# Moving two context blocks, the row order and one weight load in a 512-row gather kernel

## The chip, the cores and the metric

One core of one Trainium2 chip. The metric is the device time of one execution in microseconds (us). TensorE is called PE, VectorE DVE, ScalarE ACT, GpSimd POOL and SyncE SP, as in the profile.

## The reference, cut to what matters

Two model blocks run one after the other on 256 tokens of width 1024. The first ends with a PEER layer: each token and head picks 16 experts, and for each of them a row of `u_tab` and a row of `v_tab` are fetched. The second block has two streams, the latent `x` and a context `ctx`, and a gated feed-forward layer (`_conv_ffn`) whose weights both streams share.

```python
def _peer(h, w_q, sub_keys, u_tab, v_tab):
    ...
    def block_fn(args):
        tb, ib, gb = args
        u = u_tab[ib]
        act = jax.nn.gelu(jnp.einsum("td,thkd->thk", tb, u).astype(jnp.float32), approximate=False)
        vv = v_tab[ib]
        return jnp.einsum("thk,thkd->td", (gb * act).astype(vv.dtype), vv)

def _conv_ffn(h, w_up, conv_w, conv_b, w_down):
    u = h @ w_up
    up = jnp.pad(u, ((0, 0), (1, 1), (0, 0)))
    u = up[:, :-2] * conv_w[0] + up[:, 1:-1] * conv_w[1] + up[:, 2:] * conv_w[2] + conv_b
    a, v = jnp.split(u, 2, axis=-1)
    return (jax.nn.silu(a) * v) @ w_down
```

## The kernel before

**The gathers.** The PEER layer is 512 indirect DMAs issued by POOL (line 3099). Each brings 128 table rows of 4 KB (0.524 MB) into one of `NR = 12` ring buffers; below, one such DMA is called a row. There are 256 u rows (two token tiles of 128) and 256 v rows (eight segments of 32; the first 128 belong to token tile 0). The list `ROWS` (`fetched`, line 365) sets their order. A buffer is used again when its row has been consumed: a u row by one DVE dot product (`tensor_tensor_reduce`, line 2031), v rows by PE. PE takes v rows of tile 0 two at a time and those of tile 1 four at a time (`beside_others`); here a *v group* is four v rows of tile 1, taken by eight 512-column matmuls.

**What is woven into them.** `woven` (line 461) walks through the row order on PE, DVE and ACT alike, and at places counted in rows it advances a second program, `context()`, by one step. `step_places` (line 484) is the table of these places. A row is consumed 11 rows after it is issued, and six counts come ahead of the first row, so a step at place P comes when the rows up to number P - 18 have been consumed.

**The context program.** It computes the context stream's pool mixer and feed-forward layer and, as the weights are in SBUF anyway, the first 119 tokens of x as well. A *visit* is one 128-wide block of the up-projection (two halves of 8 matmuls), its three-tap convolution (ACT line 2442 for the middle tap, then four DVE operations of `conv_up`, line 1651), a SiLU on ACT and a product on DVE. There are three kinds of visit in this stretch: `ctx` (256 context columns), `a` (120 columns of x) and `both` (377 columns, context and x at once). The `a` columns exist only when token tile 0 has finished the PEER layer: v row 128 consumed, the sum added (`v_add`), then normalised, pooled and normalised again. That part is `first_half()` below. So the first `EARLY_BLOCKS` blocks are visited twice, as `ctx` before and as `a` after it, and the other blocks once, as `both`. After the 22 blocks comes the down-projection (`cd`, 24 steps), then the context's key and value projection (weights `kvc`), and after the last v row the remaining 138 columns of x ("stage b").

In the kernel before, `ctx` visits 0 to 7 stand at places 178 to 269, `first_half()` at 292 to 316, the eight `a` visits at 318 to 334, the 14 `both` visits at 336 to 420, and `cd` at 428 to 498. `BESIDE` lists steps of `first_half()` beside which visits stand; it is empty.

**Loads.** SP issues the weight loads in program order into three slots of 2 MB and waits, before each, for the work that last used the slot. `kvc` (line 703) is behind the last down-projection load and ahead of a wait for the end of the down-projection (`p_cd`, 24).

Of the kernel before, what the change touches and what calls it, by code (L numbers as in the profile page):

```python
# [96 lines left out]
def program(nc, a, out):  # L97
# [2 lines left out]
    MUL, ADD, SUB, MAX, MIN, BYP = ALU.mult, ALU.add, ALU.subtract, ALU.max, ALU.min, ALU.bypass  # L100
    ctx = ExitStack()

    EARLY_BLOCKS, BESIDE = 8, ()

    GOES_ON = {
        "p_gp": ("p_hT", 4), "p_h2T": ("p_gp", 1), "p_xc": ("p_h2T", 4), "p_zb": ("p_xc", 4), "p_xT": ("p_zb", 1), "p_zbb": ("p_xT", 2), "p_xTb": ("p_zbb", 1), "p_cum": ("p_g", 1), "p_crow": ("p_cum", 1),
# [24 lines left out]
    def at(name, n):  # L131

        sem = S[name]
        while name in GOES_ON:
            name, before = GOES_ON[name]
            n += before
        return sem, n
# [168 lines left out]
    FIRST_B, BEFORE_A = 22 + EARLY_BLOCKS, EARLY_BLOCKS - len(BESIDE)  # L306
# [57 lines left out]
    AHEAD = 40  # L364

    def fetched():


        u = [("u", n // 128, n % 128) for n in range(256)]
        v = [("v", s, n) for s in range(8) for n in range(32)]  # L370
        first = [x for g in range(0, 128 - AHEAD, 4) for x in v[g:g + 4] + u[AHEAD + g:AHEAD + g + 4]]
        g0 = 128 - AHEAD
        first += [x for g in range(5) for x in v[g0 + 8 * g:g0 + 8 * g + 8] + u[128 + 4 * g:132 + 4 * g]]
        then = [x for g in range(20) for x in v[128 + 4 * g:132 + 4 * g] + u[176 + 4 * g:180 + 4 * g]]
        return u[0:AHEAD] + first + u[148:176] + then + v[208:]

    ROWS = fetched()
    NTH = {x: n for n, x in enumerate(ROWS)}

# [104 lines left out]
    def step_places():  # L484

        places = [5 * (k + 1) // 2 for k in range(11)] + [44 + 56 * (k - 10) // 10 for k in range(11, 34)]
        n = 178
        for f in range(BEFORE_A + 2):
            places.append(n)
            n += 13 if f < BEFORE_A else 2  # L490
        n = max(n, 292)
        for lengths in ([1.9] * 14, [2.3] * EARLY_BLOCKS, [6.4] * (22 - EARLY_BLOCKS), [1] * 2,
                        ([3.3] * 8 + [2.4] * 4) * 2, [1] * 11):
            for length in lengths:
                places.append(int(n))
                n += length
        return places
# [9 lines left out]
    def woven(peer, context):  # L507


        n, steps, half = 0, 0, None  # L510
        places = step_places()
        for what in peer:
            if what == "rest":
                n += 1
                if n == half:
                    next(context, None)
                    half = None
                elif steps < len(places) and n >= places[steps]:
                    steps += 1
                    if next(context, None) == "half":  # L520
                        half = n + 3
        for _ in context:
            pass
# [107 lines left out]
    def _(sp):  # L631
        free, count, nth = [None] * 4, [0] * 4, [0]

        def load(name, until, *parts, n=4, slot=None):

            i = nth[0] % n if slot is None else slot
            nth[0] += 1
            for signal in free[i] or ():
                sp.wait_ge(*at(*signal))
            for put, src in parts:  # L640
                sp.dma_start(put(slots[i]), src).then_inc(S[f"d_w{i}"], 16)
                count[i] += 16
            free[i] = until if isinstance(until, list) else [until]
            ready[name] = S[f"d_w{i}"], count[i], slots[i]

        def kcols(w, c0, n):
            return ((lambda ap: ap[:, 0:8 * n].rearrange("p (k c) -> p k c", k=8)),
                    w[:, c0:c0 + n].rearrange("(k p) c -> p k c", p=128))
# [8 lines left out]
        def down(l, half, f0, nf):  # L657
            w = a["ffn_w_down_2"][l]
            return ((lambda ap: ap[:, 0:512 * nf].rearrange("p (f c) -> p f c", f=nf)),
                    w[128 * f0:128 * (f0 + nf), 512 * half:512 * half + 512].rearrange("(f p) c -> p f c", p=128))  # L660
# [42 lines left out]
        for half in range(2):  # L703
            for q, (f0, nf) in enumerate(((0, 8), (8, 8), (16, 6))):
                load(("cdn", half, q), ("p_cd", 4 * (3 * half + q) + 4), down(0, half, f0, nf), n=3)
        load("kvc", ("p_ckv", 3), kcols(a["attn_w_qkv_2"][0], 1024, 512), n=3)
        sp.wait_ge(*at("p_cd", 24))
        sp.dma_start(cl[:, 0:512], a["c_late"][:, 0:512]).then_inc(S["d_l"], 16)
        sp.dma_start(hpC[:, 0:1568], a["c_bands"]).then_inc(S["d_l"], 16)
        sp.dma_start(nfb, a["normf_g"].partition_broadcast(128)).then_inc(S["d_g2"], 16)  # L710
        nth[0] = 0
        sp.wait_ge(*at("p_v", 248))
        load("pool", ("p_pl", 4), pool_w(), n=3)
# [916 lines left out]
    def _(ve):  # L1630
# [381 lines left out]
        def peer():  # L2012
            for what in turns():
# [9 lines left out]
                elif what[0] == "use" and ROWS[what[1]][0] == "u":  # L2023
                    n = what[1]
                    _, t, m = ROWS[n]
                    j, k = 8 * t + m // 16, m % 16
                    if j > 1 and k == 0:
# [1137 lines left out]
```

## Time and profile before

| | |
|---|---|
| median of 2 runs | 1694.42 us (1694.03 to 1694.82) |
| the profiled execution | 1694.82 us |
| its span | 1693.0 us, so 1.8 us lie around it |
| stretch of the gathers | first issue at 312.93 us, last at 1191.26 us |
| mean granted PE clock | 0.94 |

In the profile every f32 matmul of the program stands as two PE instructions, so one visit of 16 matmuls is x32. A timeline row merges neighbours of one form. PE times overlap a little at the seams. Times inside the program are counted from the start of the span.

### The profile page before, as it was taken

What the parts mean: (1) busy time and instruction counts of PE and PEld (TensorE: products, weight loads), DVE (VectorE), ACT (ScalarE), POOL (GpSimd) and SP (SyncE); (2) the same over time, 40 slices, a digit from 0 to 9 for tenths busy, and PEclk for the clock granted to TensorE, in tenths of its full rate; (3) what the DMA queues carried; (4) which work ended last, traced back from release to release, by engine and by line L of the source; (5) the groups of instructions that cost most, each with busy time, mean ns of one, the idle gap of its engine ahead of it and who ended that gap; (6) DMA issues with size and microseconds to landing.
All of it is one profiled execution on the core that took longest, in us unless ns stands there. A gap on an engine that the chain in (4) does not pass through costs nothing.

```text
span 1693.0 us, 22384 instructions
## 1 busy us (share of the span) xinstructions
PE 1464.2 (86%) x8446; PEld 1037.2 (61%) x8446; DVE 1041.1 (61%) x2200; ACT 530.3 (31%) x836; POOL 748.3 (44%) x676
## 2 busy tenths in 40 slices
PE   8999999827676769743999989998699999999999
PEld 7997675824121334323755545555399986699987
DVE  4865633897597866489787774401244157568864
ACT  6653331211121121132331220003233164466652
POOL 0025220477677777675566556643100013027650
PEclk9999999978778889876999999998899999999999
DMA  7447860799999999998999999986768756635451
GB/s 277 150 150 314 320 225 25 261 396 332 399 400 385 375 391 405 394 402 306 361 398 401 370 353 359 372 320 237 250 219 278 265 215 264 211 138 188 174 194 43
DMA packets 160267, 487.40 MB, mean 288 GB/s; under 512 B 10144, under 2 KB 13984, under 8 KB 156960
## 3 DMA queue, kind: packets, MB, share of 16 engines
q0 software_dynamic: 73728, 268.47, 41.4%
q1 hardware_dynamic: 86432, 217.51, 35.2%
q8 instruction: 67, 1.10, 0.3%
q14 instruction: 40, 0.33, 0.1%
HBM read 484.89 MB, written 1.05 MB: 287 GB/s over the span
## 4 chain that ended last, share of the span: by engine, by line
PE 55%; DVE 15%; DMA 9%; POOL 7%; issue 6%; ACT 2%; DVEq 0%; ACTq 0%; POOLq 0%
PE ps L764 54%; POOL arena L3099 6%; DMA arena<-in_peer_v,cl 5%; DVE arena L2031 4%; DMA arena<-in_peer_u,arena 3%; DVE arena L1645 2%; PE ps L768 2%; DVE wring L2031 1%; DVE arena L1651 1%; POOL wring L3099 1%; DVE cbase L1651 1%; ACT arena L2442 1%; DVE arena L1648 1%; DMA wring<-in_peer_u,arena 1%; DMA wring<-in_attn_w_qkv 0%
## 5 line engine op out<-in xcount | busy, mean ns | idle before, releaser
L764 PE MATMUL ps<-arena,wring 128*32 128x512 f32 (+6 forms) x3016 | 697.9, 467 | 111.0 <-DMA arena<-in_peer_v,cl 77.8
L764 PEld LDWEIGHTS ps<-arena,wring 128*128 128x128 f32 (+1 forms) x3016 | 395.5, 171 | 396.4 <-DMA arena<-in_peer_v,cl 138.6
L3099 POOL DMA_INDIRECT arena<-in_peer_u,arena x206 | 236.2, 1147 | 218.4 <-DVE arena L1988 77.4
L2031 DVE CUSTOM_DVE_ANT_0 arena<-arena 128x1024 f32<-128x1024 f32 x206 | 246.7, 1225 | 122.8 <-DMA arena<-in_peer_u,arena 119.7
L3099 POOL DMA_INDIRECT arena<-in_peer_v,cl x222 | 240.1, 1081 | 132.7 <-issue 59.4
L2442 ACT ACT_TABLE_LOAD x71 | 91.1, 1283 | 355.6 <-DVE arena L2031 178.2
L1651 DVE SCALAR_TENSOR_TENSOR cvs<-ps,vec,cvs 128x255 f32<-128x255 f32 (+3 forms) x236 | 104.5, 443 | 55.2 <-ACT cvs L2442 47.9
L764 PE MATMUL ps<-hhl,wh 128*128 128x256 f32 (+1 forms) x528 | 126.2, 322 | 0.6 <-POOL hhl L3109 0.4
L764 PEld LDWEIGHTS ps<-arena 128*128 128x128 f32 (+1 forms) x708 | 87.6, 196 | 45.9 <-issue 27.5
L1645 DVE TENSOR_TENSOR wl<-wring,wh 128x2048 fp32r<-128x2048 f32 (+1 forms) x42 | 92.5, 2202 | 37.0 <-ACT wh L2445 36.1
L764 PE MATMUL ps<-arena 128*128 128x128 f32 (+4 forms) x708 | 99.1, 293 | 18.3 <-DVE arena L1648 6.4
L3053 POOL TENSOR_TENSOR arena<-arena,cl 128x256 f32<-128x256 f32 x56 | 43.8, 782 | 158.0 <-PE ps L764 154.7
L2445 ACT ACTIVATE wh<-wring 128x2048 fp32r<-128x2048 f32 (+1 forms) x44 | 82.6, 1878 | 70.7 <-PE ps L764 36.7
L764 PE MATMUL ps<-ahl,wh 128*128 128x512 f32 (+1 forms) x320 | 103.0, 347 | 0.1
L2445 ACT ACTIVATE arena<-ps 128x512 f32<-128x512 f32 (+1 forms) x97 | 56.0, 578 | 145.1 <-PE ps L764 105.1
L764 PE MATMUL ps<-hhl,wl 128*128 128x256 f32 x352 | 99.2, 282 | 0.0
L764 PEld LDWEIGHTS ps<-hhl,wh 128*128 128x128 f32 x528 | 87.8, 190 | 9.8 <-POOL hhl L3109 1.3
L2442 ACT ACTIVATE arena<-arena 128x16 f32<-128x16 f32 (+3 forms) x60 | 35.4, 591 | 182.3 <-DVE arena L2031 57.2
L764 PE MATMUL ps<-sqb,wring 128*128 128x138 f32 (+1 forms) x736 | 89.5, 285 | 2.1 <-ACT xT L2442 2.1
L764 PEld LDWEIGHTS ps<-sqb,wring 128*128 128x128 f32 x736 | 88.5, 193 | 3.0 <-issue 2.3
L2442 ACT ACTIVATE cvs<-ps,vec 128x256 f32<-128x256 f32 (+3 forms) x118 | 62.9, 533 | 80.4 <-PE ps L764 65.5
L3125 POOL TENSOR_TENSOR wl<-wring,wh 128x2048 fp32r<-128x2048 f32 x3 | 13.7, 4574 | 160.9 <-ACT wh L2445 160.7
(279 smaller groups left out, 2208.9 us busy)
## 6 DMA issues: line engine op xcount, KB each, us to landing
wring<-in_ups SPq DMA_DIRECT2D x37, 2048.0 KB, 9.7
wring<-in_ada SPq DMA_DIRECT2D x24, 2048.0 KB, 10.1
wring<-in_ffn_w_down SPq DMA_DIRECT2D x12, 2048.0 KB, 7.8
wring<-in_w_in SPq DMA_DIRECT2D x8, 2048.0 KB, 8.3
wring<-in_ffn_w_down SPq DMA_DIRECT2D x6, 1536.0 KB, 6.8
wring<-in_peer_wq SPq DMA_DIRECT2D x4, 2048.0 KB, 15.8
wring<-in_attn_w_qkv SPq DMA_DIRECT2D x4, 2048.0 KB, 8.5
wring<-in_w_out SPq DMA_DIRECT2D x2, 2048.0 KB, 9.3
```

Of the source, the lines that this page charges most:

```text
L764: return pe.matmul(o, l, r, start=start, stop=stop)
L768: return pe.transpose(o, i, ident[0:n, 0:n])
L1645: return ve.tensor_tensor(o, x, y, op)
L1648: return ve.tensor_scalar(o, x, s1, s2, op0, op1)
L1651: return ve.scalar_tensor_tensor(o, x, s, y, op0, op1)
L2031: ve.tensor_tensor_reduce(out=o, in0=o, in1=h2[:, t, :], scale=1.0, scalar=0.0, op0=MUL, op1=ADD, accum_out=dots[j % 2][:, k:k + 1]).then_ ...
L2442: return ac.activation(o, x, f, bias=bias, scale=scale, accum_out=accum)
L2445: return ac.activation(o, x, ACT.Copy)
L3053: k = po.tensor_tensor(OTs[l % 2][:, m:m + 2, :], AM[:, m:m + 2, :], bc(cl[:, o:o + 128], 2, 1), MUL)
L3099: po.indirect_dma_start(out=ring[n % NR], out_offset=None, in_=table, in_offset=bass.IndirectOffsetOnAxis(ap=which, axis=0)).then_inc(S[f" ...
L3125: told(po.tensor_tensor(lo.bitcast(FR), src, hi, SUB), *split_done(n))
```

## The change

It does four things. (1) The row order is regular: after the first 40 u rows it alternates 4 v rows and 4 u rows until the u rows end, and 40 v rows are left. Before, there was a piece with 8 v rows to 4 u rows and then 28 u rows alone, and 48 v rows were left. (2) Two more blocks are early ones: 10 `ctx` and 10 `a` visits, 12 `both` visits. (3) Four of the `ctx` visits (6 to 9) stand beside steps 0, 1, 8 and 9 of `first_half()`; the table of places is changed for that: `ctx` 0 to 5 at places 178 to 278, `first_half()` at 311 to 326, `a` at 327 to 348, `both` at 350 to 421, `cd` at 430 to 498. (4) The load `kvc` is issued after the wait for the end of the down-projection and three small loads.

```diff
-    EARLY_BLOCKS, BESIDE = 8, ()
+    EARLY_BLOCKS, BESIDE = 10, (0, 1, 8, 9)
...
-        first = [x for g in range(0, 128 - AHEAD, 4) for x in v[g:g + 4] + u[AHEAD + g:AHEAD + g + 4]]
-        g0 = 128 - AHEAD
-        first += [x for g in range(5) for x in v[g0 + 8 * g:g0 + 8 * g + 8] + u[128 + 4 * g:132 + 4 * g]]
-        then = [x for g in range(20) for x in v[128 + 4 * g:132 + 4 * g] + u[176 + 4 * g:180 + 4 * g]]
-        return u[0:AHEAD] + first + u[148:176] + then + v[208:]
+        both = [x for g in range(0, 256 - AHEAD, 4) for x in v[g:g + 4] + u[AHEAD + g:AHEAD + g + 4]]
+        return u[0:AHEAD] + both + v[256 - AHEAD:]
...
-            n += 13 if f < BEFORE_A else 2
-        n = max(n, 292)
+            n += 20 if f < BEFORE_A else 2
+        n = max(n, 311)
...
-        load("kvc", ("p_ckv", 3), kcols(a["attn_w_qkv_2"][0], 1024, 512), n=3)
         sp.wait_ge(*at("p_cd", 24))
         sp.dma_start(cl[:, 0:512], a["c_late"][:, 0:512]).then_inc(S["d_l"], 16)
         sp.dma_start(hpC[:, 0:1568], a["c_bands"]).then_inc(S["d_l"], 16)
         sp.dma_start(nfb, a["normf_g"].partition_broadcast(128)).then_inc(S["d_g2"], 16)
+        load("kvc", ("p_ckv", 3), kcols(a["attn_w_qkv_2"][0], 1024, 512), n=3)
```

PE's order around `first_half()` before. 32x512 is a matmul on a v row, 128x256 (x16) a `ctx` visit, the 128x120 rows on `cbase` and `wring` x16 belong to `first_half()`, and 128x120 x16 per visit after them are the `a` visits:

```order
L764 MATMUL ps<-arena,wring 32x512 x28
L764 MATMUL ps<-arena,cbase 128x120 x4
L768 MATMUL ps<-cbase,arena 128x128 x8
L764 MATMUL ps<-arena 128x136 x8
L764 MATMUL ps<-arena,wring 128x120 x16
L768 MATMUL ps<-cbase,gt 128x128
L764 MATMUL ps<-arena,cbase 128x120 x8
L768 MATMUL ps<-cbase,wt 128x128
L764 MATMUL ps<-arena,wring 128x120 x48
L764 MATMUL ps<-arena,wring 32x512 x8
```

The same piece of PE's order in the changed kernel:

```order
L761 MATMUL ps<-arena,cbase 128x120 x4
L761 MATMUL ps<-arena,wring 128x256 x32
L765 MATMUL ps<-cbase,arena 128x128 x8
L761 MATMUL ps<-arena 128x136 x8
...
L761 MATMUL ps<-arena,wring 128x120 x8
L761 MATMUL ps<-arena,wring 128x256 x16
L761 MATMUL ps<-arena,cbase 128x120 x8
L761 MATMUL ps<-arena,wring 128x256 x16
L761 MATMUL ps<-arena,wring 32x512 x8
L761 MATMUL ps<-arena,wring 128x120 x48
```

Two whole `ctx` visits now stand between the first piece of `first_half()` and its transposes, and one on either side of its last sum; a v group stands behind them.

SP's order at the end of the down-projection, before:

```order
L641 DMA wring<-in_ffn_w_down 128x6x512
L641 DMA wring<-in_attn_w_qkv 128x8x512
L708 DMA cl<-in_c_late 128x512
L709 DMA arena<-in_c_bands 128x1568
L710 DMA arena<-in_normf_g 128x1024
```

and in the changed kernel:

```order
L638 DMA wring<-in_ffn_w_down 128x6x512
L704 DMA cl<-in_c_late 128x512
L705 DMA arena<-in_c_bands 128x1568
L706 DMA arena<-in_normf_g 128x1024
L638 DMA wring<-in_attn_w_qkv 128x8x512
```

The 2 MB of `in_attn_w_qkv` (`kvc`) have moved behind the wait that stands at `in_c_late` and behind that load and the next two.

## Rows read from the trace of the kernel before

**Rows 1.** The page: engine totals, and clock and DMA share in 40 slices.

```profile
PE 1464.2 (86%) x8446; PEld 1037.2 (61%) x8446; DVE 1041.1 (61%) x2200; ACT 530.3 (31%) x836; POOL 748.3 (44%) x676
...
PEclk9999999978778889876999999998899999999999
DMA  7447860799999999998999999986768756635451
```

**Rows 2.** Windows: busy time of each engine in seven stretches.

```profile
core 0: us, PE busy (x) PEld busy (x) DVE busy (x) ACT busy (x) POOL busy (x), PEclk, DMA share, GB/s
590.70:731.00 140.30, 104.02 (x426) 51.63 (x424) 86.30 (x210) 22.72 (x35) 99.90 (x94) 0.91 1.02 395
731.00:743.00 12.00, 11.19 (x31) 2.09 (x30) 9.14 (x26) 4.48 (x8) 8.95 (x11) 0.82 1.03 406
743.00:799.40 56.40, 17.06 (x83) 15.24 (x82) 54.25 (x133) 17.67 (x39) 36.53 (x29) 0.64 0.92 339
799.40:835.00 35.60, 34.92 (x288) 31.63 (x288) 27.53 (x78) 11.47 (x21) 16.50 (x15) 0.94 0.95 343
835.00:1000.00 165.00, 163.34 (x616) 87.02 (x617) 128.36 (x292) 44.44 (x69) 101.06 (x90) 1.00 1.01 388
1000.00:1144.10 144.10, 139.75 (x547) 73.32 (x549) 52.18 (x105) 4.38 (x8) 81.80 (x80) 0.99 0.94 347
1144.10:1202.00 57.90, 42.53 (x218) 23.08 (x222) 7.41 (x15) 14.32 (x26) 19.71 (x21) 0.91 0.74 269
```

**Rows 3.** The chain that ended last, inside first_half: start us, us, what.

```profile
784.19 3.52 DVE arena L2031 x7
...
788.53 2.38 DVE arena L2031 x4
```

**Rows 4.** Timeline of PE: one ctx visit, then the matmuls of first_half.

```profile
669.58 7.08 PE L764 MATMUL ps<-arena,wring 128*128 128x256 f32 x32
...
743.07 1.15 PE L764 MATMUL ps<-arena,cbase 128*128 128x120 f32 x8
756.99 1.97 PE L768 MATMUL ps<-cbase,arena 128*128 128x128 f32 x8 [12.77 <-DVE arena L1648]
...
784.04 3.74 PE L764 MATMUL ps<-arena,cbase 128*128 128x120 f32 x16 [2.23 <-ACT arena L2442]
```

**Rows 5.** DVE in 743 to 799.4 us, by line: busy, mean ns.

```profile
L2031 DVE CUSTOM_DVE_ANT_0 arena<-arena 128x1024 f32<-128x1024 f32 x22 | 26.1, 1223 | 0.4
L2031 DVE CUSTOM_DVE_ANT_0 wring<-wring,arena 128x1024 f32<-128x1024 f32 x4 | 4.8, 1226 | 0.1
```

**Rows 6.** Timeline of DVE: product and taps of ctx visits.

```profile
732.36 0.43 DVE L1645 TENSOR_TENSOR arena<-cvs 128x256 f32<-128x256 f32 x1 [1.69 <-ACT cvs L2442]
733.56 2.04 DVE L1651 SCALAR_TENSOR_TENSOR cbase<-ps,vec,cbase 128x255 f32<-128x255 f32 x4 [0.77 <-ACT cbase L2442]
```

**Rows 7.** PE by form, 799.4 to 835 us (a visits), then 835 to 1000 us.

```profile
L764 PE MATMUL ps<-arena,wring 128*128 128x120 f32 x256 | 31.4, 287 | 7.6 <-ACT arena L2442 7.6
...
L764 PE MATMUL ps<-arena,wring 128*128 128x377 f32 x438 | 142.3, 482 | 0.7 <-DMA wring<-in_ups 0.7
```

**Rows 8.** The page's DMA issues: the up-projection weights, KB each, us to landing.

```profile
wring<-in_ups SPq DMA_DIRECT2D x37, 2048.0 KB, 9.7
```

**Rows 9.** Timeline of PE behind the down-projection: a v group, the first key projection.

```profile
1150.81 1.92 PE L764 MATMUL ps<-arena,wring 128*32 128x512 f32 x16
1159.61 10.02 PE L764 MATMUL ps<-arena,wring 128*128 128x256 f32 x32 [6.87 <-issue]
```

**Rows 10.** Timeline of SP's queue: the kvc load and the last load behind the wait.

```profile
1098.33 0.37 SPq L641 DMA_DIRECT2D wring<-in_attn_w_qkv  x1
...
1144.97 0.65 SPq L710 DMA_DIRECT2D arena<-in_normf_g  x1
```

**Rows 11.** DMA view, 1144.1 to 1202 us: share in 40 slices, one issue and its us to landing.

```profile
DMA  9999999999999300000000389986899899999999
...
arena<-in_normf_g SPq DMA_DIRECT2D x1, 512.0 KB, 11.2
```

More of the change, by code:

```diff
@@ L489, in step_places @@
             places.append(n)
-            n += 13 if f < BEFORE_A else 2
-        n = max(n, 292)
-        for lengths in ([1.9] * 14, [2.3] * EARLY_BLOCKS, [6.4] * (22 - EARLY_BLOCKS), [1] * 2,
-                        ([3.3] * 8 + [2.4] * 4) * 2, [1] * 11):
+            n += 20 if f < BEFORE_A else 2
+        n = max(n, 311)
+        for lengths in ([1.2] * 14, [2.3] * EARLY_BLOCKS, [6.4] * (22 - EARLY_BLOCKS), [1.5] * 2,
+                        ([3.2] * 8 + [2.4] * 4) * 2, [1] * 11):
             for length in lengths:
```

## The prediction

> **What bounds the kernel now.** I read the page's totals and slices first. PE is busy 86% of the span, and where its clock falls, around 340 to 480 us and again near 760 to 800 us, the DMA share is high: the gathers, not PE, set the pace there [rows 1]. Then the windows, cut at the borders of the steps [rows 2]. They show four regimes. Up to 743 us the DMA engines are full (share 1.02 and 1.03, 395 to 406 GB/s), and PE has slack: 104 of 140 us. From 743 to 799.4 us, the steps of first_half, PE works 17.06 of 56.4 us at a clock of 0.64, the DMA share falls to 0.92 with 339 GB/s, and DVE is busy 54.25 us: DVE is the bound. From 799.4 to 1144.1 us (a visits, both visits, down-projection) PE is busy 338.0 of 344.7 us: PE is the bound, and what counts there is the amount of matmul work. In the last stretch, up to the last v row at about 1202 us, PE and DMA alternate.
>
> The chain of waits agrees for the second regime: it runs through u row products on DVE, one behind the other [rows 3]. There are 26 of them in that stretch, 30.9 us of DVE's 54.25 [rows 5], since 28 u rows stand alone there. PE meanwhile has four waits between short pieces, the longest 12.77 us for DVE's scaled rows [rows 4].
>
> **Part 1, where first_half starts: +21 us.** It needs the last v row of tile 0 and place 292 or 311. Counted in ROWS, that v row is number 271 before and number 291 after, 20 rows later. Up to it DMA is the bound in both kernels: the windows show 395 GB/s, so a row of 0.524 MB costs 1.33 us, and 20 rows 26.5 us. Against that, SP has fewer loads to make before that point. Before, the slots allow one load of the last two early weight pairs, the pool weights and two pairs for both visits; after, both remaining early pairs and the pool weights, but no pair for later, as these slots are freed only by ctx visits 6 to 9. That is one load of 2.1 MB less, 5.3 us. Net 26.5 - 5.3 = +21.2, and first_half starts at 743 + 21 = 764 us. Bounds: 0 (if the two ctx visits taken away from here had held it back; PE's slack speaks against it) and 30 (20 rows at the 1.5 us a row of the windows' 94 issues in 140.3 us). The two ctx visits that leave this stretch save nothing: PE has 36 us of slack in it.
>
> **Part 2, the length of first_half: -3 us.** PE's own 17.06 us remain. The four ctx visits at 7.08 us each [rows 4] add 28.3 us. Placed end to end that is 45.4 us, the lower bound; if nothing overlapped, 56.4 + 28.3 = 84.7 us, the upper. On DVE the 26 u products shrink to about 9, as only 16 places pass and half the rows are v rows: -17 x 1.19 = -20 us. Taps and product of a ctx visit add 2.04 + 0.43 us [rows 6], four times 9.9 us. So DVE falls to about 44 us and is no longer alone the bound. Step by step: PE does its first 1.15 us, then visits 6 and 7, 15 us, which covers the 12.77 us wait almost exactly. Transposes, windows and pool matmuls follow, waiting for DVE and ACT by turns, to about 26 us; visit 8, sum, visit 9 bring PE to about 42 us. Behind visit 9 stand ACT's middle tap, DVE's 2.04 us of taps, then the reciprocal and eight scalings and ACT's eight shifts before the first a visit may start, since DVE takes the taps of visit 9 ahead of the scalings: about 11 us of PE waiting are left. I take 53 us against 56.4, nearest to the lower bound because the two long waits are covered: -3.4 us. The a visits start at 764 + 53 = 817 us instead of 799.4.
>
> **Part 3, the PE-bound stretch: -17 us.** Two more a visits: 31.4 us for eight is 3.92 us each [rows 7], +7.8 us. Two both visits fewer: 142.3 us for 438 instructions is 0.325 us, times 32 is 10.4 us a visit [rows 7], -20.8 us. v groups consumed between the first a visit and the end of the down-projection: 24 before (rows 307 to 479), 22 after (315 to 479, without 471), as two of them fall into first_half, where PE waits anyway. At 1.92 us [rows 9] that is -3.8 us. The down-projection itself does not change. Sum -16.8 us. Bounds: -22 (ten a visits in 34 us, since some of the eight ran while the clock was still at its lower level; it averages 0.94 there [rows 2]) and 0 (the loads below come late). DMA has room over the whole stretch: about 170 rows and 28 MB of weights, 117 MB, need 296 us at 395 GB/s, and PE needs 327.
>
> The weights of the a visits are the cover that gets thin. The pair for a visits 2 and 3 and that for 4 and 5 are issued only when visit 9 has left PE, about 11 us before the first a visit; the first of them is wanted 8 us after that, the second after another 10 us. The median load of this kind lands in 9.7 us [rows 8], about half of these gaps, so I cost it at nothing, and at up to 10 us if gathers fill the DMA engines at that time.
>
> **Part 4, the kvc load: +6 us.** Before, it is issued at 1098.33 us, long before its first use at 1159.61 us [rows 9, 10]. After, it stands behind p_cd 24 and three loads, so behind 1144.97 us [rows 10]; in front of it the 512 KB gain takes 11.2 us to land, at 1156.2 us [rows 11]. The DMA engines are full until about slice 13 of that window, 1163 us, and then stand idle for 12 us [rows 11]. With 2.1 MB more, 5.2 us at 405 GB/s, they empty at about 1168.5 us, and the load is in by then: PE waits 0 to 9 us beyond 1159.6. I take 6. PE is in order: behind this wait stand the v groups whose buffers the last 12 gathers need, so all of the wait goes to the end. The wait also keeps nothing back on SP: the pool weights behind it are gated by p_v 248 later on.
>
> The Trainium skill says in "DMA: Bandwidth & Descriptors", section "Queues, rings and completion order", that each DMA engine alternates between the queues that have work. By that rule kvc would have half of the 405 GB/s from 1156.2 us on, an estimate of 10.4 us, landing at 1166.6 us, a wait of 7 us; the full drain gives 9, and an undisturbed load none. The trace shows only the totals here.
>
> **The sum.** +21.2 - 3.4 - 16.8 + 6 = +7.0 us. On the profiled execution, 1694.8 us (span 1693.0 and 1.8 around it), that is 1701.8; that execution lies 0.4 us above the median, so 1701.
>
> **The rivals.**
>
> Filled better (faster). first_half shrinks to about 45.4 us (every wait covered), kvc lands in time, and the a visits run at full clock. Then the terms are +21.2 - 11 - 19 + 0 = -9: 1686 us. For it: PE's waits are in fact the 39 us that four visits of 7.08 us fit into. Against: taps of visit 9 stand ahead of the scalings on DVE, and the load has only 15 us between issue and use.
>
> Low clock in first_half (slower than before). In the stretch 743 to 799.4 us the granted clock is 0.64, so most of it at the lower level, 1.2 GHz [rows 2]. If the ctx visits placed there run at that level too, they take 14 us each instead of 7: +28 us, of which the 11 us wait behind visit 9 absorbs some. first_half is then about 70 us, and the result 1701 + 17 = 1718 us. It decides from the point where PE's waits between the pieces stay long enough for the clock to stay down. For it: even in the 12 us ahead of first_half the clock averages only 0.82. Against: two visits stand back to back for 14 us, and from 799.4 us on, with PE busy throughout, the clock averages 0.94, then 1.00 [rows 2].
>
> The Trainium skill's page "TensorE: Matmul & The Clock Gate", section "HAM oscillation — how this bites in real kernels", holds that waits between short bursts of matmuls put the next burst back to half rate. By that rule first_half of the kernel before is such a case, which its 0.64 bears out, and the new order stands between the two cases: this rival's 1718 us, or the forecast.
>
> Weights late in the a visits (slower). Five pairs, 10.5 MB, and the rows from about 320 to 350 and those refilling the ring, 28 rows or 14.7 MB, fall between visit 9 and the first both visit. At 395 GB/s that is 64 us, where PE needs 11 + 39 + 6 = 56 us. Then 8 to 10 us more: 1710 us. Against: DMA had a share of only 0.95 in the same stretch before.
>
> Nothing moved: the start of first_half shifts less than 21 us because the 8 to 4 piece was itself held up by DVE; worth at most 10 us, in the forecast's range.
>
> **How the numbers follow.** The forecast (net of a later start, a filled gap and a late load) has 0.5, its own range 1694 to 1707 us. Filled better has 0.25, 1680 to 1693. Weights late 0.12, low clock 0.13. 1684 to 1718 leaves out about 0.1 on either side. A measurement of this kernel can tell about 2% (34 us) from no change. Faster by more than that, under 1660.5 us, would need all of first_half's idle and the late start gone at once: 0.04. Slower, over 1728.3 us, needs low clock and late weights together: 0.04. Within 2%: 0.92.
>
> **What would show it.** In the profile of the changed kernel: the first 128x120 matmul on cbase near 764 us, not 743; 128x256 visits in the gap behind it at about 7 us each (14 would be the low clock); the first a visit near 817 us; waits for `wring<-in_ups` inside the a visits under 3 us in total; the first both visit near 865 us, the end of the down-projection near 1145 us; and a wait for `wring<-in_attn_w_qkv` of about 6 us ahead of the key projection. If first_half starts before 755 us or lasts under 48 us, parts 1 or 2 are wrong and the time falls below 1694.

## The result, and the profile after

The changed kernel takes 1717.45 us (median of 2 runs, 1716.17 to 1718.74) where the kernel before takes 1694.42. The ratio is 1.0146, 95% interval [1.0115, 1.0177]: 23 us slower, inside the 2% that counts as no change, but three times the 7 us of the forecast and almost at the end of its range. The profiled execution took 1717.8 us, with a span of 1715.9.

Totals, clock and DMA share on the page of the kernel after, to be held against [rows 1]. The totals say nothing: PE has 2.7 us more, in 23 us more of span. The 7 and the 6 that the clock had in the eighteenth and nineteenth slice are now 8 and 9: first_half is filled.

```profile
PE 1466.9 (85%) x8510; PEld 1041.6 (61%) x8510; DVE 1043.7 (61%) x2210; ACT 533.2 (31%) x843; POOL 742.4 (43%) x676
...
PEclk9999999968798888989899999998999999999999
DMA  7438851799999999997999997975758757545551
```

Windows of the kernel after, cut at the same steps as [rows 2]: up to first_half; first_half; the a visits; both visits and down-projection; up to the key projection; from there to shortly before the last v rows.

```profile
core 0: us, PE busy (x) PEld busy (x) DVE busy (x) ACT busy (x) POOL busy (x), PEclk, DMA share, GB/s
590.70:766.60 175.90, 115.38 (x405) 47.64 (x406) 126.46 (x307) 25.99 (x40) 130.58 (x124) 0.84 1.03 402
766.60:820.70 54.10, 41.62 (x242) 33.97 (x241) 38.30 (x100) 23.22 (x48) 20.19 (x19) 0.93 0.82 293
820.70:873.60 52.90, 46.62 (x369) 41.71 (x369) 40.09 (x101) 17.78 (x37) 26.33 (x23) 0.91 1.01 375
873.60:1158.50 284.90, 277.94 (x1049) 148.36 (x1053) 157.51 (x348) 41.19 (x60) 160.37 (x150) 0.98 0.93 350
1158.50:1184.70 26.20, 7.39 (x49) 3.71 (x46) 7.11 (x14) 7.73 (x11) 8.40 (x9) 0.74 0.95 360
```

Ahead of first_half the DMA engines are still full (1.03) and PE still has slack, 60 us of it. In first_half PE now works 41.6 of 54.1 us at a clock of 0.93, where it was 17.06 of 56.4 at 0.64; DMA falls to 0.82. The a visits take 52.9 us with the DMA engines full again.

The timeline of PE in the kernel after, first_half to the first both visit. The two ctx visits at the start of first_half run end to end, 14.0 us, and cover the old wait of 12.77 us; behind the last of them PE waits 10.34 us for ACT. Two waits for up-projection weights follow, one inside the a visits and one ahead of the first both visit.

```profile
766.57 1.06 PE L761 MATMUL ps<-arena,cbase 128*128 128x120 f32 x8
767.46 13.99 PE L761 MATMUL ps<-arena,wring 128*128 128x256 f32 x64
...
799.64 1.94 PE L761 MATMUL ps<-arena,cbase 128*128 128x120 f32 x16
801.41 8.94 PE L761 MATMUL ps<-arena,wring 128*128 128x256 f32 x48
820.70 27.08 PE L761 MATMUL ps<-arena,wring 128*128 128x120 f32 x210 [10.34 <-ACT arena L2439]
...
859.22 10.89 PE L761 MATMUL ps<-arena,wring 128*128 128x120 f32 x80 [2.80 <-DMA wring<-in_ups]
873.58 2.16 PE L761 MATMUL ps<-arena,wring 128*128 128x377 f32 x4 [3.48 <-DMA wring<-in_ups]
```

Further on, still PE of the kernel after: the first key projection and the stage that follows the last v row.

```profile
1165.19 1.92 PE L761 MATMUL ps<-arena,wring 128*32 128x512 f32 x16
1184.66 9.00 PE L761 MATMUL ps<-arena,wring 128*128 128x256 f32 x32 [17.55 <-DMA wring<-in_attn_w_qkv]
...
1233.68 3.97 PE L761 MATMUL ps<-arena 128*128 128x136 f32 x16 [6.29 <-DVE arena L1645]
```

In the kernel before that last stage starts at 1209.42 us and the key projection at 1159.61 [rows 9]. Six marks hold the whole story (start times on PE, us; the down-projection by its end):

| | first_half | a visits | first both visit | down-projection ends | key projection | stage after the last v row |
|---|---|---|---|---|---|---|
| before | 743.1 | 799.4 | 835.0 | 1144.1 | 1159.6 | 1209.4 |
| after | 766.6 | 820.7 | 873.6 | 1158.5 | 1184.7 | 1233.7 |
| stage, after less before | +23.5 | -2.3 | +17.3 | -24.2 | +10.7 | -0.8 |

The last line is the change of the stretch that ends at each mark (the first one: of all that lies ahead of first_half). It adds up to 24.2 us; the spans differ by 22.9.

### The profile page after: what moved, and what is told of

Same layout as the page of the kernel before. It is cut to its first block, busy times and chain, and to the rows that moved or that the text cites. A ratio compares the mean times of both kernels' runs of the same rounds, so it can differ in the third digit from the quotient of the medians.

```text
span 1715.9 us, 22539 instructions
## 1 busy us (share of the span) xinstructions
PE 1466.9 (85%) x8510; PEld 1041.6 (61%) x8510; DVE 1043.7 (61%) x2210; ACT 533.2 (31%) x843; POOL 742.4 (43%) x676
## 4 chain that ended last, share of the span: by engine, by line
PE 57%; DMA 11%; POOL 10%; DVE 9%; issue 5%; ACT 2%; SPq 0%; DVEq 0%; ACTq 0%; POOLq 0%
PE ps L761 56%; POOL arena L3096 8%; DMA arena<-in_peer_v,cl 3%; DMA wring<-in_peer_v,cl 2%; POOL wring L3096 2%; DMA arena<-in_peer_u,arena 2%; DVE arena L2028 2%; DMA wring<-in_ups 2%; PE ps L765 1%; DMA wring<-in_attn_w_qkv 1%; DVE arena L1642 1%; DVE arena L1648 1%; ACT arena L2439 1%; DMA wring<-in_peer_u,arena 1%; DVE cbase L1648 0%
## 5 line engine op out<-in xcount | busy, mean ns | idle before, releaser
L761 PEld LDWEIGHTS ps<-arena,wring 128*128 128x128 f32 (+1 forms) x3048 | 404.6, 173 | 422.9 <-DMA arena<-in_peer_v,cl 169.2
L3096 POOL DMA_INDIRECT arena<-in_peer_u,arena x214 | 243.7, 1139 | 256.8 <-PE ps L761 117.0
L2028 DVE CUSTOM_DVE_ANT_0 arena<-arena 128x1024 f32<-128x1024 f32 x214 | 256.9, 1224 | 123.3 <-DMA arena<-in_peer_u,arena 120.0
L3096 POOL DMA_INDIRECT arena<-in_peer_v,cl x214 | 231.6, 1082 | 131.4 <-issue 59.2
```

The lines of the kernel that those rows point to most:

```text
L761: return pe.matmul(o, l, r, start=start, stop=stop)
L2028: ve.tensor_tensor_reduce(out=o, in0=o, in1=h2[:, t, :], scale=1.0, scalar=0.0, op0=MUL, op1=ADD, accum_out=dots[j % 2][:, k:k + 1]).then_ ...
L3096: po.indirect_dma_start(out=ring[n % NR], out_offset=None, in_=table, in_offset=bass.IndirectOffsetOnAxis(ap=which, axis=0)).then_inc(S[f" ...
```

## The experiments

Sixteen runs of fifteen kernels (one kernel ran twice) stand in four sets; each set shares its runs of the kernel before, whose medians were 1704.9, 1697.0, 1694.8 and 1696.9 us. Absolute times are compared inside a set only, ratios across them. Two words for what follows: "kvc early" means the load in its place of before, and a "place" is a number in the step table, by which steps are spread over the list of rows.

**First set: the parts of the change by themselves.** Theory A came from the marks: the late kvc load and the later start of first_half make the loss, while the ten early blocks give something back. Its rival C was that the visits inside first_half lose.

The kernel before with the kvc load moved behind the wait, and nothing else:

```diff
-        load("kvc", ("p_ckv", 3), kcols(a["attn_w_qkv_2"][0], 1024, 512), n=3)
         sp.wait_ge(*at("p_cd", 24))
...
         sp.dma_start(nfb, a["normf_g"].partition_broadcast(128)).then_inc(S["d_g2"], 16)
+        load("kvc", ("p_ckv", 3), kcols(a["attn_w_qkv_2"][0], 1024, 512), n=3)
```

> The kernel before with part 4 alone: kvc issued behind the wait for the end of the down-projection and the three small loads. Theory A (the load's lateness is on the path, since PE's wait for it holds back the v groups and with them the last gathers): PE waits 15 to 18 us ahead of the key projection instead of 6.9, and the time is 9 to 12 us longer, 1704 to 1707. Rival B (the end is set by gathers and the wait is hidden): within 2 us of before, 1693 to 1697.

Ratio 1.006 [1.0037, 1.0084], 10 us. The wait ahead of the key projection, in the timeline of PE of this kernel:

```profile
1173.65 6.72 PE L764 MATMUL ps<-arena,wring 128*128 128x256 f32 x21 [18.59 <-DMA wring<-in_attn_w_qkv]
```

18.59 us instead of 6.87, and the 11.7 us more go to the end almost whole.

The kernel after with that one line back in its old place:

> The changed kernel with part 4 undone: kvc issued ahead of the wait, as before. Theory A: 1717.5 minus 9 to 12, 1705 to 1709, of which the rest over before comes from the later start. Rival B: 1716 to 1719.

Ratio 1.0084 [1.0052, 1.0117], 0.6% under the 1.0146 of the kernel after. The same price from the other side. The wait at the key projection is back to what it was:

```profile
1189.07 3.33 PE L761 MATMUL ps<-arena,wring 128*128 128x256 f32 x7 [6.88 <-issue]
```

The kernel before with the regular row order and the places that go with it, but 8 early blocks, none in first_half, kvc early:

```diff
-        first = [x for g in range(0, 128 - AHEAD, 4) for x in v[g:g + 4] + u[AHEAD + g:AHEAD + g + 4]]
...
-        return u[0:AHEAD] + first + u[148:176] + then + v[208:]
+        both = [x for g in range(0, 256 - AHEAD, 4) for x in v[g:g + 4] + u[AHEAD + g:AHEAD + g + 4]]
+        return u[0:AHEAD] + both + v[256 - AHEAD:]
...
-        n = max(n, 292)
+        n = max(n, 311)
-        for lengths in ([1.9] * 14, [2.3] * EARLY_BLOCKS, [6.4] * (22 - EARLY_BLOCKS), [1] * 2,
-                        ([3.3] * 8 + [2.4] * 4) * 2, [1] * 11):
+        for lengths in ([1.2] * 14, [2.3] * EARLY_BLOCKS, [6.4] * (22 - EARLY_BLOCKS), [1.5] * 2,
+                        ([3.2] * 8 + [2.4] * 4) * 2, [1] * 11):
```

> The kernel before with the regular row order and the table of places that it needs (first_half at 311, its steps 1.2 apart, down-projection as in the changed kernel), still 8 early blocks, all ctx visits ahead of first_half, kvc early. Theory A (first_half waits for the last v row of tile 0, 20 rows later, and what is lost there is only partly won back by fewer u products inside it): first_half starts near 766 us, lasts 38 to 42 us, so the a visits start near 806 us instead of 799, and the time is 1696 to 1702. Rival C (the visits placed in first_half and their late weights cause the loss, the order does not): 1690 to 1695.

Ratio 0.9949 [0.993, 0.9968]: faster than before, and than either theory had it, though first_half starts 20 places later. Theory A's account of the late start fell here. first_half took 36 us (before: 56.4), and, what nobody had counted on, the stretch from the key projection to the stage after the last v row took 31.8 us where the kernel before takes 49.8.

The kernel before with the other half of the change, `EARLY_BLOCKS, BESIDE = 10, (0, 1, 8, 9)`, and the old row order:

> The kernel before with part 2 and 3 of the change alone: 10 early blocks, ctx visits 6 to 9 beside steps 0, 1, 8 and 9 of first_half, everything else (row order, table's numbers, kvc) as before. Theory A: first_half starts at 743 us as before, takes about 64 us as DVE is its bound and gets 10 us more, and the PE-bound stretch is 13 us shorter: 1684 to 1692. Rival C (visits in first_half cost more than they cover, by late weights): 1698 to 1710.

Ratio 1.01 [1.0065, 1.0135], slower, as rival C had it. first_half took 83 us. It still held the 28 u rows that stand alone in the old order, and the four visits came on top, with waits of 8.59, 6.79, 5.11 and 8.02 us between the pieces. The new order does not rescue the four visits either: 1.0084 with both against 0.9949 with the order alone.

**Second set: the number of early blocks or their place?**

The kernel after, kvc early, `EARLY_BLOCKS, BESIDE = 8, (0, 1, 8, 9)`:

> The kernel after with the kvc load early and with 8 early blocks instead of 10, all four visits still placed inside first_half (BESIDE stays). Theory P (the place is what costs: visits inside first_half lengthen DVE's and ACT's line there and free the weight slots late, so that the a visits start late and run slowly): the ratio to before stays at 1.005 to 1.015, first_half lasts 50 us or more. Theory N (the number is what costs: two more early blocks need more visits ahead of first_half and two more a visits): the ratio falls to that of the kernel with the order alone, 0.995, within 0.003.

Ratio 0.9984 [0.9968, 1.0001]. The same, `10, ()` and 12 places between the visits:

> The kernel after with the kvc load early, 10 early blocks, and BESIDE empty: all ten ctx visits stand ahead of first_half, 12 places apart. Theory P (place): PE has slack there and two both visits (20.8 us) become two a visits (7.8 us), so it is faster than the order alone: ratio 0.985 to 0.993. Theory N (number): the ten visits hold the stretch ahead of first_half up, ratio 1.003 or more.

Ratio 0.9993 [0.998, 1.0006]. The kernel before with ten blocks ahead of first_half, 11 places apart:

> The kernel before with 10 early blocks, 11 places apart instead of 13, all ahead of first_half, first_half still at place 292, the old row order. Theory P: 8 to 13 us faster than before, ratio 0.992 to 0.996. Theory N: no faster, ratio 0.999 or more.

Ratio 0.9984 [0.9967, 1.0001]. And the kernel after (kvc late) with `8, ()` and 13 places:

> The kernel after (kvc late) with 8 early blocks ahead of first_half and BESIDE empty, so that the row order, its places and the late kvc load are what is left of the change. If the parts add, it has the order's 0.995 and kvc's 0.006: 1.001, between 0.998 and 1.004. If the late kvc load costs more with the new order, because the last v groups come later there, 1.005 or more.

Ratio 0.9996 [0.9981, 1.0011]; less the load's 0.006 that is 0.994, near the 0.9949 of the order alone, so these two parts add. Neither theory P nor theory N held. The place costs 0.35% (0.9984 against 0.9949), the number 0.45% (0.9993), and both together 1.35% (1.0084), more than their sum; the last of these ratios comes from the first set, the other two from the second.

Why the number costs anything was the riddle: by the marks of the kernel with ten blocks ahead of first_half, the down-projection ends at 1148.2 us, 6.8 us ahead of the one with eight (1155.0), and yet its last stage comes no earlier (1213.4 and 1212.9 us), although its kvc load is early and the other's late. The kernel before with ten blocks shows it best, in its windows: first_half, the a visits, both visits and down-projection, the rest up to the stage after the last v row.

```profile
749.00:808.70 59.70, 17.68 (x84) 16.03 (x83) 57.37 (x138) 18.07 (x40) 36.10 (x29) 0.58 0.92 342
808.70:859.80 51.10, 46.11 (x369) 41.21 (x369) 42.04 (x115) 16.28 (x33) 25.43 (x24) 0.92 0.98 361
859.80:1134.80 275.00, 273.30 (x1048) 145.98 (x1048) 163.37 (x360) 41.41 (x63) 162.78 (x151) 1.00 0.99 376
1134.80:1207.80 73.00, 52.21 (x257) 24.59 (x257) 11.43 (x24) 17.30 (x32) 27.46 (x30) 0.94 0.82 302
```

The down-projection ends at 1134.8 instead of 1144.1 us, 9.3 us earlier, and the last window grows from 65.3 to 73.0, in which PE works only 52. The gain is given back to waits for rows.

**Third set: what the tail waits for.** The timeline of POOL of the kernel before, which issues the gathers, holds the cause. The first row of a run of four gathers names what it waited for:

```profile
1152.99 0.94 POOL L3099 DMA_INDIRECT arena<-in_peer_v,cl  x1 [2.14 <-PE ps L764]
...
1156.74 0.94 POOL L3099 DMA_INDIRECT arena<-in_peer_v,cl  x1 [0.30 <-issue]
1175.19 0.94 POOL L3099 DMA_INDIRECT arena<-in_peer_v,cl  x1 [17.50 <-PE ps L764]
...
1182.55 0.94 POOL L3099 DMA_INDIRECT arena<-in_peer_v,cl  x1 [2.69 <-PE ps L764]
...
1191.26 0.94 POOL L3099 DMA_INDIRECT arena<-in_peer_v,cl  x1 [0.31 <-issue]
```

Behind 1156.74 us no buffer is free until PE, in its order, is through the key projection and the v group behind it: 17.5 us without an issue. Twelve gathers are still to come after that, and PE ends up waiting for them. Its waits between the key projection and the last stage, in the kernel before:

```profile
PE ps L764 <- DMA arena<-in_peer_v,cl: 6.5, 7, 1.6
PE ps L764 <- DMA wring<-in_peer_v,cl: 0.7, 1, 0.7
```

That is 7.2 us in eight waits. How many are left is set by the place at which the down-projection ends, and that is a sum of the table. The order alone ends it at place 509 (311 + 14 x 1.2 + 8 x 2.3 + 14 x 6.4 + 2 x 1.5 + 70.4), the kernel after at 501, since two both visits of 6.4 fewer and two a visits of 2.3 more are 8 places. The kernel before ends it at 501 too, by its own table (292 + 14 x 1.9 + 8 x 2.3 + 14 x 6.4 + 2 x 1 + 72). Theory G: this, not the matmul work, decides.

The kernel before with one number changed:

```diff
-        for lengths in ([1.9] * 14, [2.3] * EARLY_BLOCKS, [6.4] * (22 - EARLY_BLOCKS), [1] * 2,
+        for lengths in ([1.9] * 14, [2.3] * EARLY_BLOCKS, [7.0] * (22 - EARLY_BLOCKS), [1] * 2,
```

> The kernel before with the both visits 7.0 places apart instead of 6.4: the down-projection ends at place 508 instead of 500, and nothing else changes. Theory G (the gathers set the end of this stretch; PE finishes the down-projection early and then waits while the last v rows come): with 8 rows fewer left behind the key projection, the stretch from the key projection to the stage after the last v row falls from 49.8 to 30 to 40 us, while the end of the down-projection moves by at most 8 us; ratio 0.993 to 0.998. Theory M (PE's matmul work from 799 to 1144 us sets the end, as in the prediction): v groups only change their place, ratio 0.999 to 1.003.

Ratio 0.9949 [0.9932, 0.9966]. The whole gain of the new order, from one number. PE of this kernel, key projection and last stage, then the first and the last of POOL's last four gathers:

```profile
1167.87 9.48 PE L764 MATMUL ps<-arena,wring 128*128 128x256 f32 x32 [6.88 <-issue]
...
1189.83 4.21 PE L764 MATMUL ps<-arena,wring 128*32 128x512 f32 x32
1199.98 2.38 PE L764 MATMUL ps<-arena 128*128 128x136 f32 x9 [5.94 <-DVE arena L1648]
```

```profile
1182.91 0.94 POOL L3099 DMA_INDIRECT arena<-in_peer_v,cl  x1 [16.98 <-PE ps L764]
...
1186.63 0.93 POOL L3099 DMA_INDIRECT arena<-in_peer_v,cl  x1 [0.31 <-issue]
```

The key projection comes 8.3 us later (8 more rows are used ahead of it), four gathers are left instead of twelve, and from there to the last stage it is 32.1 us instead of 49.8. The gap on POOL is as long as it was, but little is left behind it. PE has no wait for rows in this stretch any more, and its busy time there falls by 10.5 us (36.64 to 26.16), of which two v groups less are 3.8; the rest is not accounted for.

The kernel after, with 7.1 in the place of 6.4:

> The kernel after with the both visits 7.1 places apart instead of 6.4, so that the down-projection ends at place 509 instead of 501; the rest of the change stays, the late kvc load too. Theory G: the two both visits taken away brought the down-projection's end 8 places forward, and the rows left over come behind it; given back, the ratio falls from 1.0146 to about 1.010. Theory M: the same ratio as after, within 0.002.

Ratio 1.0072 [1.0052, 1.0091]: half of the change's loss was this, and more than theory G had forecast (1.010). The down-projection ends 4.2 us later (1162.7), the last stage comes 13.4 us earlier (1220.3).

New order, kvc early, ten blocks all ahead of first_half, 7.1:

> The kernel with the new row order, kvc early, ten ctx visits ahead of first_half (ratio 0.9993 with 6.4) and the both visits 7.1 places apart. Theory G: 4 to 8 us less, ratio 0.994 to 0.997. Theory M: 0.998 to 1.001.

Ratio 0.9927 [0.9908, 0.9946], 1682.05 us against 1694.79, faster than both kernels of this case and the fastest that ran. From 0.9993 that is 0.66%, some 11 us where theory G had 4 to 8: its direction holds, its size was again too small. And the order alone once more, to see whether its gain hung on the chip:

> The same kernel as the one with the regular row order and its places alone (8 early blocks, BESIDE empty, kvc early), on another chip. If its 0.9949 was no accident of that chip: 0.992 to 0.997. An accident: 0.999 or more.

0.9945 [0.9928, 0.9962]; it did not.

Theory G in all eighteen traces (the stretch is from the key projection to the last stage; "gathers left" are those that POOL issues after the key projection has begun; some of these kernels come in the fourth set):

| kernel | down-projection ends at place | gathers left | stretch, us |
|---|---|---|---|
| before with ten blocks ahead of first_half | 492 | 20 | 57.4 |
| before with ten blocks, four inside first_half | 492 | 20 | 55.2 |
| before; the same with kvc late | 501 | 12 | 49.8; 48.7 |
| after; the same with kvc early | 501 | 12 | 49.0; 49.4 |
| new order, ten blocks ahead of first_half | 501 | 12 | 49.7 |
| before with 7.0 | 509 | 4 | 32.1 |
| after with 7.1 | 509 | 4 | 32.0 |
| new order, eight blocks (two runs; with kvc late) | 509 | 4 | 31.8 and 31.7; 31.3 |
| new order, eight blocks, four inside first_half | 509 | 4 | 31.7 |
| new order, ten blocks, 7.1 (none, two, two or four inside first_half) | 509 | 4 | 32.0, 31.7, 32.0, 32.0 |
| new order, ten blocks, 7.8 | 518 | 0 | 30.2 |

The stretch follows the gathers left and hardly anything else that was varied, neither the row order nor the number of blocks, the place of the visits or the kvc load. It does not follow them in proportion: from 4 to 12 it grows by 17 to 18 us, from 12 to 20 by only 6 to 8.

**Fourth set: which visits inside first_half cost.** All with the new order, kvc early, ten blocks and 7.1. All four inside:

> The kernel after with the kvc load early and the both visits 7.1 places apart: of the change, the row order, ten early blocks and the four visits inside first_half are left. If the parts add (1.0072 for the wide one, less 0.006 for the load): ratio 0.999 to 1.003. What remains above the 0.9927 of the same kernel with all ten visits ahead of first_half is the price of the place of the visits.

Ratio 1.0004 [0.999, 1.0018], so the place of four visits is worth 0.77% here. Only the two at the start of first_half (`(0, 1)`, 15 places between the others):

> As the one with kvc early and 7.1, but only visits 8 and 9 inside first_half, at its first two steps, and eight ahead of it, 15 places apart. Theory W (a visit inside first_half costs where nothing waits: these two fall into the wait of 10 us for DVE's scaled rows, which they cover): first_half lasts 36 to 44 us, ratio 0.992 to 0.996. Theory S (each visit inside first_half costs about the same, for PE has slack ahead of it and none in it): half of the price, ratio 0.995 to 0.999.

Ratio 0.9938 [0.9922, 0.9955]. Only the two at its end (`(8, 9)`):

> As the one before, but visits 8 and 9 at first_half's last steps, beside and behind the sum. Theory W: here is the price: the wait for ACT ahead of the first a visit stays at 10.3 us, the one for DVE's scaled rows comes back, first_half lasts 45 to 52 us, ratio 0.998 to 1.002. Theory S: half of the price, 0.995 to 0.999.

Ratio 0.9961 [0.9949, 0.9973]. The first two are nearly free (0.11% above 0.9927, within the intervals), the last two cost 0.34%. Theory W had length and ratio of the first kernel and the waits and the length of the second, but not its ratio (0.998 to 1.002); that one lies in the range of theory S. So W holds in its direction, and not in its size. PE's timeline of the kernel with `(8, 9)` has both waits, the one that is not covered any more and the one that these visits make.

```profile
780.71 1.97 PE L765 MATMUL ps<-cbase,arena 128*128 128x128 f32 x8 [9.69 <-DVE arena L1645]
...
819.47 2.91 PE L761 MATMUL ps<-arena,wring 128*128 128x120 f32 x12 [10.34 <-ACT arena L2439]
```

With `(0, 1)` the first is almost gone, and the second is only 6.45 us:

```profile
786.34 1.09 PE L765 MATMUL ps<-cbase,arena 128*128 128x128 f32 x8 [0.58 <-DVE arena L1645]
...
811.10 1.21 PE L761 MATMUL ps<-arena,wring 128*128 128x120 f32 x4 [6.45 <-ACT arena L2439]
```

first_half lasts 33.3 us with no visit in it, 40.2 with the first two, 49.5 with the last two, 54.2 with four, and it starts only 1.6, 2.5 and 3.6 us earlier for them. Together they cost more (0.77%) than one by one (0.11 and 0.34%); by the traces the surplus does not arise in first_half (20.9 us longer for 6.9 and 16.2) but behind it: from the first a visit to the end of the down-projection it is 342.4 us with four visits inside, 340.6 with none, and 339.6 and 337.8 with two. Why is open. The windows of the four-visit kernel show the DMA engines at 0.80 and 284 GB/s over the longer first_half, so that more loads and rows are left for the stretch behind; that this is the reason is not shown:

```profile
768.90:823.10 54.20, 41.70 (x242) 34.05 (x241) 38.40 (x100) 23.22 (x48) 20.19 (x19) 0.95 0.80 284
```

Last, the fastest version with 7.8 instead of 7.1, so that the down-projection ends near place 518:

> The version that is fastest so far (new row order, kvc early, ten visits ahead of first_half, both visits 7.1 apart: 0.9927) with 7.8 instead, so that the down-projection ends at place 517 and all rows are gathered by then. Theory G (the gathers set the end): the tail behind the key projection loses nothing more, since its 32 us are PE's own work by then; ratio 0.991 to 0.995. If there were still rows to gain: under 0.990. If PE now waits for rows inside the down-projection: 0.996 or more.

Ratio 0.9936 [0.9916, 0.9956], no different from 0.9927. The last gather is issued at 1161.32 us, ahead of the key projection at 1171.04. Once four gathers or fewer are left, PE's own 30 to 32 us are the tail.

## Why the prediction was wrong, by its own steps

**Part 1, the start of first_half: right.** Forecast +21.2, measured +23.5 (766.6 for 764). What it was added up from stood too: 301 gathers were issued from 312 us to first_half instead of 281, and five loads of up-projection weights instead of six.

**Part 2, its length: right as a number.** 54.1 us for 53; -2.3 for -3.4. The steps stood too: visits at 7.0 us and full clock, the 12.77 us wait covered, "about 11 us of PE waiting" behind the last visit, 10.34 measured. DVE had 9 u products in it, as forecast. The low-clock rival is out: the stretch has 0.93, and 1.00 over the first two visits (767.4 to 781.5 us). That its 1718 us is the measured time is an accident. But the comparison misled. That first_half did not grow against 56.4 looked like four visits for nothing. The new order without them has a first_half of 33 to 36 us; the change won some 20 us there and spent them again on visits that PE's slack ahead of first_half had carried for next to nothing. The fourth set prices that at 0.77%.

**Part 3, the PE-bound stretch: this step failed first.** Forecast -16.8, measured -6.9 (17.3 - 24.2). Its terms give the a visits 35.6 + 7.8 = 43.4 us and what follows -20.8 - 3.8 = -24.6. The mark of 865 us for the first both visit was reckoned wrong, for 817 + 43.4 is 860.4. Measured are 52.9 us and -24.2: of the 9.9 us that are missing, 9.5 lie in the a visits, and the saving behind them nearly came. PE in the a visits of the kernel after, by form:

```profile
L761 PE MATMUL ps<-arena,wring 128*128 128x120 f32 x320 | 41.2, 296 | 13.1 <-ACT arena L2439 10.3 <-DMA wring<-in_ups 2.8
...
L761 PE MATMUL ps<-arena,wring 128*128 128x377 f32 x1 | 0.6, 584 | 3.5 <-DMA wring<-in_ups 3.5
```

The waits for weights are 2.80 + 3.48 = 6.3 us where the kernel before has 0.7, so 5.6 of the 9.5 us. Another 2.0 are the ten visits' own time, 41.2 for 39.2: behind its wait of 10.34 us PE runs the first 9.3 us of them at a granted clock of 0.68, where the kernel before has 0.80 over the first 10.6 us, behind a wait of 7.59. The last 1.9 are a third v group in this stretch where there were two (48 instructions of 128x512 for 32); counted where it stands, it leaves the stretch behind 2.3 us short of its saving.

The term that failed is "I cost it at nothing" for the weight loads. It rested on a median landing time of 9.7 us over the whole program [rows 8]. In the very stretch of interest the DMA view of the kernel after says:

```profile
wring<-in_ups SPq DMA_DIRECT2D x5, 2048.0 KB, 26.3
```

and that of the kernel before, from 799.4 to 835 us, had said already:

```profile
wring<-in_ups SPq DMA_DIRECT2D x4, 2048.0 KB, 20.2
```

Two and three times the median of the page, and the waits came to 6.3 us, not "under 3". They are not those that the prediction looked at. The two pairs that wait for visit 9 were issued from 808.53 us on, landed after 11.4 and 21.5 us, and came in time. Late are two that were issued inside the a visits, at 840.11 and 847.26 us: they landed after 19.1 and 26.3 us, at 859.2 and 873.6, where PE's two waits end. Nor do they hang on the visits inside first_half: with the new order and ten visits ahead of it the same waits come to 8.5 and 8.7 us (6.4 and 7.1 places), with the kernel before and ten blocks to 5.0. The rival of late weights had the right account: 64 us from the end of visit 9 to the first both visit, for 56 in the forecast. It was 63.2 us (810.4 to 873.6), at a DMA share of 1.01, and the rival's chance of 0.12 was too small.

**Part 4, the kvc load: right mechanism, size too small.** Forecast +6, measured +10.7 in the trace (17.55 us of waiting for 6.87), and 0.6% in two experiments from both sides (0.5% and 0.7% between two more pairs of kernels that differ in it alone). Full drain had been put at 9 us and was the right case, but 6 was taken: the DMA engines stayed full until about 1183 us, and the load was in at 1184.6. From the DMA view of the kernel after:

```profile
wring<-in_attn_w_qkv SPq DMA_DIRECT2D x1, 2048.0 KB, 24.7
```

The load was issued at 1159.88 us, behind three others on its own queue, of which the last landed at 1170.4 us; eight more gathers were issued meanwhile, from 1160.56 to 1171.12 us. The Trainium skill's rule that a DMA engine alternates between its queues packet by packet ("DMA: Bandwidth & Descriptors", "Queues, rings and completion order") stands behind the prediction's estimate: half of the rate, 10.4 us from the landing of the 512 KB gain on, and 7 us of wait. The DMA view of the kernel after from 1170.4 to 1184.7 us (packets, MB, share) shows how it came out:

```profile
DMA packets 1856, 5.20 MB, mean 364 GB/s; under 512 B 128, under 2 KB 128, under 8 KB 1856
...
q0 software_dynamic: 924, 3.33, 58.7%
q1 hardware_dynamic: 932, 1.88, 34.3%
```

q0 carries the gathers and q1 the load. Counted in packets they had nearly the same, 924 and 932, which agrees with that rule. But a packet of the gathers moved 3.6 KB and one of the load 2.0 KB, so the load had 36% of the bytes and took 14.2 us for the 10.4 of the estimate. Those 3.8 us are about what the 7 us lack of the measured 10.7.

**The sum.** The four misses, 2.3 + 1.1 + 9.9 + 4.7 us, less 0.8 in the tail, are the 17 us between +7 and +24 of the marks.

**What the sum left out.** It let everything up to the key projection go to the end one for one and took the 49.8 us behind as fixed. In the trace they stayed (49.0), but by cancelling: the new order's places end the down-projection 8 places further on, worth -18 us there, and two both visits fewer take the 8 places back. The prediction saw "the v groups whose buffers the last 12 gathers need" and drew only one consequence from it, that kvc's wait goes to the end. The other, that an earlier end of the down-projection leaves rows behind, is what ate the saving of PE work: ten early blocks ahead of first_half gave next to nothing with 6.4 in the old order (0.9984) and cost 0.45% in the new one (0.9993 for 0.9949), and with 7.1 they gave 0.2% beyond the order alone (0.9927 for 0.9945, the intervals overlap). Of the rivals, "Filled better" needed every wait of first_half covered, kvc in time and quick weights, and had none of the three.

The parts by ratio, as the runs have them: row order and its places -0.5%, late kvc load +0.6%, ten early blocks +0.45% (from the rows they leave behind), the visits inside first_half +0.9% on top. That is 1.45%, against 1.46% measured. The agreement proves little, since these are steps of one chain of kernels (0.9949, 0.9993, 1.0084, 1.0146), in which only the price of the load was also taken by itself; and the first step is not the row order's own, as one number in the table of the kernel before gives the same 0.9949.

## What to carry to other kernels

Where PE and gathers feed each other through a ring of buffers, count how many gathers are still to be issued when PE reaches a long piece that frees none: eight fewer there were worth 0.5% by one number in a table, while 9 us less of PE time ahead of it were worth next to nothing. Read the landing time of a load in the stretch where the new load will run, not the median of the page. And before filling a wait on the bound engine, ask what the same piece costs where it stands: work moved out of an engine's slack into its critical stretch is not free because the stretch kept its old length.

## What the hardware showed that was not expected

A 2 MB weight load took 9.4 us to land as the page's median, 20.2 and 26.3 us in stretches at a DMA share of 0.95 to 1.01 with gathers on the other queue, and up to 31.5 us for one of them. The visits inside first_half, in pieces of 9 to 14 us with other work and waits of up to 10.34 us around them, brought PE's granted clock there from 0.64 to 0.93. While a 2 MB load and gathers shared full DMA engines, both queues moved nearly the same number of packets (932 and 924 in 14.3 us), and the one with packets of 2.0 KB got 36% of the bytes. That is one stretch: in the kernel before, from 820 to 835 us and with engines as full, the counts were 1464 and 814, and why is not shown. And the same kernel before had medians from 1694.4 to 1704.9 us in the different sets, 0.6%, so that half-per-cent effects could only be read from ratios inside a set.
